# The last two convolution tiles, the layer norm and two output units of a conformer module, each done in two token streams on one core

## The chip, the cores and the metric

One core of a Trainium2 chip runs the whole program in one launch. The metric is device time in microseconds (us), the median of the runs.

## The reference, cut to what matters

The reference is a chain of transformer blocks at 256 tokens and width 1024. The change lies in layer 1 of the second block, which runs a conformer module over two sequences with shared weights: the latents and the context. They stand side by side as 512 columns, and this text calls each half of 256 columns a stream.

```python
def conformer_conv(h, w1, b1, dw, dwb, ln_g, ln_b, w2, b2):
    u = h @ w1 + b1
    a, g = jnp.split(u, 2, axis=-1)
    u = a * jax.nn.sigmoid(g)
    u = dwconv(u, dw) + dwb            # depthwise, 31 taps
    u = jax.nn.silu(layernorm(u, ln_g, ln_b))
    return u @ w2 + b2
```

## The kernel before, in words

**Layout.** Activations lie feature-major: 1024 features are 8 tiles (KT = 8) of 128 partitions, and the free axis holds 512 tokens, stream 0 in columns 0 to 255 and stream 1 in 256 to 511. A product keeps nearly full f32 accuracy with three matmuls per tile of the contraction (lines 1149 to 1151): weight hi with input hi, weight hi with input lo, weight lo with input hi. The weights come in units of 1024 by 256. SP loads a unit into one of 3 raw buffers; ACT makes its hi half in two pieces (L1359, L1360), and DVE the lo half (L1656, L1659). hi and lo have 2 slots, so unit j+2 can be split only when PE has finished with unit j.

**Order.** A planner written in Python (class Plan) writes one list of steps, and every engine goes through it in order and takes its own part of each step. So the list's order is each engine's queue. `beside` (L341) adds a share of `pace` to a credit after each tile of a product and, at 1, puts in one `condition` step (L329): 2 reductions of 1.2 us on DVE (L1735) over a buffer MW, which POOL loads anew after each. There are 192 such steps in the program, and later layers need their results.

**Depthwise convolution** (`cv_conv`, L1318). Per feature tile, copies of the padded input, shifted by 0 to 3 columns, lie on the four partition groups of UX; 16 DMAs per tile make them (`cv_spread`, and for tiles 6 and 7 `cv_spread_one`, 8 on SP and 8 on POOL). PE then does 8 taps for each of 4 groups of 32 output channels, 512 columns wide, in f32. ACT adds the bias into CV (L1581), DVE sums the tiles into SA (`cv_total`, L1997).

**Layer norm.** After tile 6 PE multiplies SA by a matrix of ones (L1334), after tile 7 it adds CV's last tile (L1337), and ACT copies the sum to RS as minus the mean (L1586). DVE centers the 8 tiles (L2002), ACT squares each (L1367) into one of two buffers, PE sums the squares with 8 matmuls by ones (L1179, L1182). ACT makes the reciprocal deviation by Ln and Exp (L1371, L1374), loads the table for Silu (L1352), and for each tile: DVE scales (L2007), ACT does Silu (L1591) and the hi copy (L1594), DVE the lo half (L2012).

**Output.** Four units 181 to 184 of cv_w2 give two output tiles each. ACT moves an output tile with its bias to AB (L1598), DVE adds it into the residual X (L1727), ACT squares it (L1367), POOL adds the squares into SA (L2084). The last unit, `close` (L394), runs stream 0 of both tiles, then stream 1, so that the norm of the following MLP can begin with stream 0: in the midst of stream 1 stand the two ones matmuls of stream 0 (`ones_part`, L1189 and L1192).

Of the kernel before, what the change touches and what calls it, by code (L numbers as in the profile page):

```python
# [1134 lines left out]
def tensor(e, w, m, p, acc):  # L1135
# [195 lines left out]
    def cv_total(k, u):  # L1331
        if k == KT - 2:
            w.wait_ge(("cv_add", k), free_of(6, u))
            e.matmul(m.ps[6][:, 0:512], ones, m.SA[:, :], start=True, stop=False).then_inc(*acc.says("cv_summed"))  # L1334
        if k == KT - 1:
            w.wait_ge(("cv_sum", k))
            e.matmul(m.ps[6][:, 0:512], ones, m.CV[:, k, :], start=False, stop=True).then_inc(  # L1337
                *acc.says(("acc", 6, u)))
# [893 lines left out]
```

## Time and profile before

| what | value |
|---|---|
| median of 3 runs | 3013.59 us (3011.38 to 3013.71) |
| the profiled execution's own time | 3015.04 us |
| its span, first to last instruction | 3013.1 us |
| mean granted TensorE clock | 0.985 |
| PE, DVE, ACT, POOL busy | 96%, 66%, 40%, 12% |
| the chain that ended last, by engine | PE 84%, DVE 9%, ACT 4%, DMA 1%, issue 1%, POOL 1% |

The profile is one execution; all times in it count from the start of its span. A row of the timeline gives start, length, engine, line and operation, and in brackets how long the engine was idle before and who ended that. The clock is told as a share of full speed: 1.00 is 2.4 GHz, 0.50 is 1.2 GHz.

### The profile page before, as it was taken

To read this page: it belongs to the slowest core of one execution; us is meant where nothing else is said; L and a number is where in the kernel's file an instruction comes from. 1 tells how busy PE (TensorE), PEld (TensorE's weight loads), DVE (VectorE), ACT (ScalarE), POOL (GpSimd) and SP (SyncE) were. 2 spreads that over 40 slices of the span, in tenths; PEclk is the share of its full clock that TensorE was granted. 3 is DMA by queue.
4 is the path that set the end of the run, shared out by engine and by line. 5 is a ranking of instruction groups with operands and counts; after the bars stand their busy time and mean duration, and the time that the engine had idled before them with its cause. 6 is when DMAs were issued, how large, how long until landed. Compare 5 with 4: busy or idle time off the path is not lost.

```text
span 3013.1 us, 42743 instructions
## 1 busy us (share of the span) xinstructions
PE 2899.0 (96%) x17730; PEld 2511.1 (83%) x17730; DVE 2000.8 (66%) x3252; ACT 1197.6 (40%) x1953; POOL 352.4 (12%) x545
## 2 busy tenths in 40 slices
PE   7999999989999989999999999999999999998998
PEld 7999998879977768888864888888888888876998
DVE  6776777658745557777644776777777667654665
ACT  5444444644444434223312632223234222443543
POOL 0000000000113220000122100001010000243000
PEclk9999999989999999999999999999999999999999
DMA  6444675347755523544464254553535545565453
GB/s 216 154 154 140 212 239 190 127 140 246 238 113 84 83 56 123 171 155 159 129 188 119 84 161 161 161 168 122 166 125 168 161 154 169 125 107 82 136 186 127
DMA packets 362275, 451.88 MB, mean 150 GB/s; under 512 B 12656, under 2 KB 332432, under 8 KB 362080
## 3 DMA queue, kind: packets, MB, share of 16 engines
q1 hardware_dynamic: 326976, 329.89, 33.7%
q0 software_dynamic: 34944, 118.65, 16.5%
q8 instruction: 140, 2.29, 0.3%
q10 hardware_dynamic: 160, 0.59, 0.1%
q14 instruction: 55, 0.45, 0.0%
HBM read 438.67 MB, written 1.05 MB: 146 GB/s over the span
## 4 chain that ended last, share of the span: by engine, by line
PE 84%; DVE 9%; ACT 4%; DMA 1%; issue 1%; POOL 1%; DVEq 0%; ACTq 0%; POOLq 0%
PE ps L1149 24%; PE ps L1151 24%; PE ps L1150 24%; PE ps L1327 2%; PE ps L1170 2%; PE ps L1171 1%; PE ps L1172 1%; DVE lo L1656 1%; PE ps L1314 1%; DVE NB L1690 1%; DVE lo L1659 1%; ACT hi L1359 1%; PE ps L1302 1%; PE ps L1282 1%; PE ps L1182 1%
## 5 line engine op out<-in xcount | busy, mean ns | idle before, releaser
L1149 PE MATMUL ps<-XN,hi 128*128 128x256 f32 (+1 forms) x3120 | 1037.3, 332 | 46.0 <-DVE XN L1903 11.3
L1150 PE MATMUL ps<-XN,hi 128*128 128x256 f32 (+1 forms) x3120 | 1020.1, 327 | 0.0
L1151 PE MATMUL ps<-XN,lo 128*128 128x256 f32 (+1 forms) x3120 | 1019.6, 327 | 0.0
L1149 PEld LDWEIGHTS ps<-XN,hi 128*128 128x128 f32 x3120 | 598.7, 192 | 122.4 <-issue 14.5
L1151 PEld LDWEIGHTS ps<-XN,lo 128*128 128x128 f32 x3120 | 598.9, 192 | 49.0
L1150 PEld LDWEIGHTS ps<-XN,hi 128*128 128x128 f32 x3120 | 599.4, 192 | 47.6
L1735 DVE CUSTOM_DVE_ANT_0 MX<-MW,C 128x1024 bf16<-128x1024 f32 x384 | 480.0, 1250 | 109.3 <-DMA MW<-in_mod_w 102.5
L1656 DVE TENSOR_TENSOR lo<-raw,hi 128x1024 fp32r<-128x1024 f32 (+1 forms) x313 | 383.9, 1227 | 242.7 <-ACT hi L1359 241.6
L1359 ACT ACTIVATE hi<-raw 128x1024 fp32r<-128x1024 f32 (+1 forms) x313 | 326.2, 1042 | 428.6 <-PE ps L1151 428.4
L1659 DVE TENSOR_TENSOR lo<-raw,hi 128x1024 fp32r<-128x1024 f32 (+1 forms) x313 | 380.3, 1215 | 0.0
L1149 PE MATMUL ps<-H,hi 128*128 128x512 f32 (+1 forms) x1072 | 380.2, 355 | 0.0
L1150 PE MATMUL ps<-H,hi 128*128 128x512 f32 (+1 forms) x1072 | 379.7, 354 | 0.0
L1151 PE MATMUL ps<-H,lo 128*128 128x512 f32 (+1 forms) x1072 | 379.7, 354 | 0.0
L1360 ACT ACTIVATE hi<-raw 128x1024 fp32r<-128x1024 f32 (+1 forms) x313 | 324.6, 1037 | 0.0
L2078 POOL DMA_DIRECT2D MW<-in_mod_w x192 | 103.0, 537 | 1451.0 <-DVE mod L1735 1341.6
L1150 PEld LDWEIGHTS ps<-H,hi 128*128 128x128 f32 x1072 | 202.7, 189 | 28.4
L1149 PEld LDWEIGHTS ps<-H,hi 128*128 128x128 f32 x1072 | 202.7, 189 | 28.2
L1151 PEld LDWEIGHTS ps<-H,lo 128*128 128x128 f32 x1072 | 202.7, 189 | 28.0
L1727 DVE SCALAR_TENSOR_TENSOR X<-ps,mod,X 128x256 f32<-128x256 f32 x244 | 108.2, 479 | 139.1 <-PE ps L1151 139.1
L2084 POOL TENSOR_TENSOR SA<-SA,NB 128x256 f32<-128x256 f32 (+1 forms) x69 | 70.4, 1020 | 812.5 <-ACT NB L1367 811.7
L1170 PE MATMUL ps<-hi,XN 128*128 128x256 f32 x512 | 151.5, 296 | 0.1
L1171 PE MATMUL ps<-lo,XN 128*128 128x256 f32 x512 | 145.5, 284 | 0.0
(239 smaller groups left out, 3402.8 us busy)
## 6 DMA issues: line engine op xcount, KB each, us to landing
raw<-in_mlp_w SPq DMA_DIRECT2D x128, 1024.0 KB, 5.4
MW<-in_mod_w POOLq DMA_DIRECT2D x192, 512.0 KB, 3.8
raw<-in_ffn_w_in SPq DMA_DIRECT2D x44, 1024.0 KB, 5.1
raw<-in_attn_w_in SPq DMA_DIRECT2D x36, 1024.0 KB, 4.8
raw<-in_na_wqkv SPq DMA_DIRECT2D x24, 1024.0 KB, 5.4
raw<-in_ffn_w_out SPq DMA_DIRECT2D x16, 1024.0 KB, 5.3
raw<-in_mlstm_w_in SPq DMA_DIRECT2D x12, 1024.0 KB, 5.0
raw<-in_cv_w SPq DMA_DIRECT2D x12, 1024.0 KB, 6.2
```

The source lines that it names most:

```text
L1149: e.matmul(out, whi, xhi, start=first, stop=False)
L1150: e.matmul(out, whi, xlo, start=False, stop=False)
L1151: i = e.matmul(out, wlo, xhi, start=False, stop=last)
L1170: e.matmul(out, xhi, hi[:, k, :], start=k == 0, stop=False)
L1171: e.matmul(out, xhi, lo[:, k, :], start=False, stop=False)
L1359: e.activation(hi[:, a:b], raw[:, a:b], ACT.Copy).then_inc(*high.says(("hi", j, 0)))
L1360: e.activation(hi[:, b:c], raw[:, b:c], ACT.Copy).then_inc(*high.says(("hi", j, 1)))
L1656: e.tensor_tensor(lo[:, a:b], raw[:, a:b], hi[:, a:b].bitcast(F32), ALU.subtract).then_inc(*low.says(("lo", j, 0)))
L1659: e.tensor_tensor(lo[:, b:c], raw[:, b:c], hi[:, b:c].bitcast(F32), ALU.subtract).then_inc(*low.says(("lo", j, 1), ("spent", j)))
L1727: e.scalar_tensor_tensor(out=m.X[:, j, a:b], in0=src[:, a:b], scalar=mod_of(m, gate, j, i), in1=m.X[:, j, a:b], op0=ALU.mult, op1=ALU.add) ...
L1735: e.tensor_tensor_reduce(out=m.MX[:, :], in0=m.MW[:, :], in1=m.C[:, s, :], scale=1.0, scalar=0.0, op0=ALU.mult, op1=ALU.add, accum_out=m.m ...
L2078: e.dma_start(m.MW[:, :], T["mod_w_2"][n // 48][n % 48 * P:(n % 48 + 1) * P, :]).then_inc(*sig["mw"].says(("mod_raw", n)))
```

## The change

Tiles 6 and 7 of the convolution, the mean, the centering, the squares, the variance and the normalisation are done per stream, with 256 columns each, and interleaved on PE: both tiles of stream 0, two taps of tile 6 of stream 1, the sum for the mean of stream 0, four more taps, the squares of stream 0, the last two taps, tile 7 of stream 1. Output units 181 and 182 multiply stream 0 of all tiles first (four PSUM banks held), with the mean and squares of stream 1 between, and stream 1 later. Squares go to four buffers in AB in place of two in NB. The splits of units 183 and 184 stand together ahead of the evacuation of unit 181. Units 181 and 182 now put in no condition step; `pace` in the last attention layer goes from 0.25 to 0.4. Line numbers of the new file are higher: 1210 to 1212 for 1149 to 1151, 1398 for the new convolution parts.

```diff
@@ -861,8 +861,7 @@

     def convolve(k):
         p.do("cv_conv", k, *p.bank())
-        p.do("cv_total", k, p.use(6)[1] if k == KT - 2 else p.bank_use[6])
-        p.flush()
+        p.do("cv_total", k)

     for c in range(4):
         def evac_g(t, b, u):
@@ -883,37 +882,94 @@
                 if k == KT - 4:
                     p.do("tables", LNEXP)
                 convolve(k)
-    for k in (KT - 2, KT - 1):
-        convolve(k)
-    p.sa_user = "cv_summed"
-    p.do("cv_mean", p.bank_use[6], p.rs_user)
-    for k in range(KT):
-        p.do("cv_center", k, p.norms)
-        p.square(k, 512, 1, "CV")
-        p.flush()
     p.flush()
-    p.rs_user = ("cv_center", KT - 1)
-    s = p.rstd(512)
+    used, rs_user, s = p.xn_used[1], p.rs_user, p.norms
+    p.norms += 1
+    x = ("cn", 0, 0, 512)
+
+    def unit(c):
+        j = p.take("cv_w2_2", 0, 0, KT, c * 256, 256)
+        p.reads(j, x)
+        return j
+
+    def products(j, banks, i, between):
+        for k in range(KT):
+            for t in range(2):
+                p.do("product", j, t, k, KT, banks[t], ("part", x, i), k == 0, k == KT - 1, i == 1, i == 1)
+            between(k)
+
+    def mean(i):
+        b, u = p.use(6 + i)
+        p.do("cv_mean_part", i, b, u, rs_user)
+        return b, u
+
+    def centered(i):
+        for k in range(KT):
+            p.do("cv_center_part", k, i)
+            p.do("cv_square_part", k, i)
+
+    def normed(i, ahead=2):
+        for k in range(KT + ahead):
+            if k < KT:
+                p.do("cv_norm_part", s, k, i)
+            if k >= ahead:
+                p.do("cv_silu_part", k - ahead, i, used)
+            if (k, i) == (ahead + 1, 0):
+                p.do("cv_conv_out", KT - 1, 1, *last)
+
+    j0 = unit(0)
+    left = [p.bank(), p.bank()]
+    for t in range(2):
+        p.do("cv_conv_part", KT - 2 + t, 0, 0, 8, *left[t])
+        p.do("cv_conv_out", KT - 2 + t, 0, *left[t])
+    p.do("cv_add_part", 0)
+    first, last = p.bank(), p.bank()
+    p.do("cv_conv_part", KT - 2, 1, 0, 2, *first)
+    sums = 6, p.bank_use[6] + 1
+    p.do("cv_total_part", 0, *sums)
+    mean(0)
+    p.do("cv_conv_part", KT - 2, 1, 2, 6, *first)
+    centered(0)
+    sums = p.use(6)
+    p.do("cv_ones_part", 0, 0, KT, *sums)
+    p.do("cv_conv_part", KT - 2, 1, 6, 8, *first)
+    p.do("cv_conv_out", KT - 2, 1, *first)
+    p.do("cv_add_part", 1)
+    p.do("rstd_part", s, 0, *sums, ("cv_center", KT - 1, 0))
     p.do("tables", SILU)
-    for k in range(KT + 2):
-        if k < KT:
-            p.do("cv_norm", s, k)
-        if k >= 2:
-            p.do("cv_silu", k - 2, p.last_unit)
+    p.do("cv_conv_part", KT - 1, 1, 0, 8, *last)
+    normed(0)
+    banks = [p.bank(), p.bank()], [p.bank(), p.bank()]
+    products(j0, banks[0], 0, lambda k: p.do("cv_total_part", 1, 7, p.bank_use[7] + 1) if k == 1 else None)
+    mean(1)
+    centered(1)
+    held, p.late = p.late, []
+    j1 = unit(1)
+    p.late = held + p.late
+    sums = p.use(7)
+    products(j1, banks[1], 0, lambda k: p.do("cv_ones_part", 1, 0, KT, *sums) if k == 3 else None)
     p.do("tables", LNEXP)
+    p.do("rstd_part", s, 1, *sums, ("cv_center", KT - 1, 1))
+    p.do("tables", SILU)
+    normed(1)
+    p.do("tables", LNEXP)
+    p.splits()
+    p.sa_user, p.sq_user = ("cv_totaled", 1), [("conv", KT - 1)] * 2
     p.rs_user = ("cn", 0, KT - 1)
-    for c in range(4):
-        def evac(t, b, u):
-            p.do("cv_out", 2 * c + t, t, b, u)
-            p.residual(2 * c + t, 512, (layer, 2), None, t, True)
-
-        def evac_part(j, t, i, b, u):
-            p.do("cv_out_part", j, t, i, b, u)
-
-        if c < 3:
-            p.linear("cv_w2_2", 0, 0, KT, c * 256, 256, ("cn", 0, 0, 512), evac, outer=c == 0, hold=c == 2)
-        else:
-            p.close("cv_w2_2", 0, 0, c * 256, ("cn", 0, 0, 512), (layer, 2), evac_part)
+
+    def evac(j, t, b, u):
+        p.do("cv_out", j, t, b, u)
+        p.residual(j, 512, (layer, 2), None, t, True)
+
+    def evac_part(j, t, i, b, u):
+        p.do("cv_out_part", j, t, i, b, u)
+
+    for c, j in enumerate((j0, j1)):
+        products(j, banks[c], 1, lambda k: None)
+        for t in range(2):
+            evac(2 * c + t, t, *banks[c][t])
+    p.linear("cv_w2_2", 0, 0, KT, 512, 256, x, lambda t, b, u: evac(4 + t, t, b, u), hold=True)
+    p.close("cv_w2_2", 0, 0, 768, x, (layer, 2), evac_part)


 def shortconv(p, layer):
@@ -996,7 +1052,7 @@
...
-    p.pace = 0.25
+    p.pace = 0.4
...
-        return ("xn", x[1][1], k, x[2]) if x[1][0] == "xn" else ready_of(x[1], k)
+        return (x[1][0], x[1][1], k, x[2]) if x[1][0] in ("xn", "cn") else ready_of(x[1], k)
...
+def squares_of(m, k):
+    return m.AB[:, k % 4 // 2, k % 2 * S:(k % 2 + 1) * S]
...
+    def cv_conv_part(k, i, j0, j1, b, u):
+        if j0 == 0:
+            w.wait_ge(("uxp", k), ("uxs", k), ("wd", k), free_of(b, u))
+        for j in range(j0, j1):
+            for g in range(4):
+                rows = m.UX[:, k // 2 % 2, g, k % 2, :].rearrange("p (s t) -> p s t", s=2)
+                f = e.matmul(m.ps[b][32 * g:32 * g + 32, 0:S], m.WD[:, k % 2, g * 8 + j, :],
+                             rows[:, i, 4 * j:4 * j + S], start=j == 0, stop=j == 7)
+        if j1 == 8:
+            f.then_inc(*acc.says(("acc", b, u), ("conv", k) if i else None))
+
+    def cv_total_part(i, b, u):
+        at = slice(i * S, (i + 1) * S)
+        w.wait_ge(("cv_add", KT - 2, i), free_of(b, u))
+        e.matmul(m.ps[b][:, 0:S], ones, m.SA[:, at], start=True, stop=False)
+        w.wait_ge(("cv_sum", KT - 1, i))
+        e.matmul(m.ps[b][:, 0:S], ones, m.CV[:, KT - 1, at], start=False, stop=True).then_inc(
+            *acc.says(("acc", b, u), ("cv_totaled", i)))
+
+    def cv_ones_part(i, k0, k1, b, u):
+        for k in range(k0, k1):
+            w.wait_ge(("cv_sq", k, i), free_of(b, u) if k == 0 else None)
+            e.matmul(m.ps[b][:, 0:S], ones, squares_of(m, k), start=k == 0, stop=k == KT - 1).then_inc(
+                *acc.says(("cv_ones", k, i), ("acc", b, u) if k == KT - 1 else None))

...
+    def cv_conv_out(k, i, b, u):
+        w.wait_ge(("acc", b, u))
+        e.activation(m.CV[:, k, i * S:(i + 1) * S], m.ps[b][:, 0:S], ACT.Identity,
+                     bias=param(m, "cv_dwb_2", k)).then_inc(*act.says(("free", b, u), ("cv_sum", k, i)))
+
+    def cv_mean_part(i, b, u, after):
+        w.wait_ge(("acc", b, u), after)
+        e.activation(m.RS[:, i * S:(i + 1) * S], m.ps[b][:, 0:S], ACT.Copy, scale=-1.0 / D).then_inc(
+            *act.says(("free", b, u), ("cv_mean", i)))
+
+    def cv_square_part(k, i):
+        w.wait_ge(("cv_center", k, i), ("cv_ones", k - 4, i) if k >= 4 else ("cv_ones", k + 4, 0) if i else None)
+        e.activation(squares_of(m, k), m.CV[:, k, i * S:(i + 1) * S], ACT.Square).then_inc(
+            *act.says(("cv_sq", k, i)))
+
+    def cv_silu_part(k, i, used):
+        at = slice(i * S, (i + 1) * S)
+        w.wait_ge(("cv_norm", k, i))
+        e.activation(m.CV[:, k, at], m.CV[:, k, at], ACT.Silu, bias=param(m, "cv_ln_b_2", k)).then_inc(
+            *act.says(("cv_silu", k, i)))
+        w.wait_ge(("cv_silu", k, i), used)
+        e.activation(m.XN[:, 0, k, at], m.CV[:, k, at], ACT.Copy).then_inc(*act.says(("cnhi", k, i)))

...
+    def cv_center_part(k, i):
+        at = slice(i * S, (i + 1) * S)
+        w.wait_ge(("cv_mean", i), ("cv_sum", k, i) if k >= KT - 2 else ("cv_sum", k))
+        if k == KT - 1:
+            w.wait_ge(("cv_totaled", i))
+        e.tensor_tensor(m.CV[:, k, at], m.CV[:, k, at], m.RS[:, at], ALU.add).then_inc(
+            *dve.says(("cv_center", k, i)))
+
...
```

PE's queue from convolution tile 4 on, in the module's middle, before (UX is the shifted input, NB and AB the squares, SA the sum of tiles, cst the ones):

```order
L1327 MATMUL ps<-UX,NB 32x512 x96
L1334 MATMUL ps<-SA,cst 128x512
L1327 MATMUL ps<-UX,NB 32x512 x32
L1337 MATMUL ps<-CV,cst 128x512
L1179 MATMUL ps<-SA,cst 128x512
L1182 MATMUL ps<-NB,cst 128x512 x7
L1149 MATMUL ps<-XN,hi 128x512
```

and now:

```order
L1388 MATMUL ps<-UX,NB 32x512 x64
L1398 MATMUL ps<-UX,NB 32x256 x72
L1406 MATMUL ps<-SA,cst 128x256
L1408 MATMUL ps<-CV,cst 128x256
L1398 MATMUL ps<-UX,NB 32x256 x16
L1414 MATMUL ps<-AB,cst 128x256 x8
L1398 MATMUL ps<-UX,NB 32x256 x40
L1210 MATMUL ps<-XN,hi 128x256
```

The 64 rows ahead are tiles 4 and 5. Of the 72 rows behind them 32 are tile 6 and 32 tile 7, both of stream 0, and 8 the first two taps of tile 6 of stream 1. So tile 7 moved ahead of the other stream's tile 6 and ahead of the first ones matmul.

How ACT's queue goes on behind the last Silu and hi copy, before (hi is a weight split, AB an output tile, X the residual):

```order
L1352 ACT_TABLE_LOAD
L1359 ACTIVATE hi<-raw 128x1024
L1360 ACTIVATE hi<-raw 128x1024
L1598 ACTIVATE AB<-ps,PV 128x512
L1367 ACTIVATE SA<-X 128x512
L1598 ACTIVATE AB<-ps,PV 128x512
L1367 ACTIVATE NB<-X 128x512
L1359 ACTIVATE hi<-raw 128x1024
```

and now:

```order
L1430 ACT_TABLE_LOAD
L1437 ACTIVATE hi<-raw 128x1024
L1438 ACTIVATE hi<-raw 128x1024
L1437 ACTIVATE hi<-raw 128x1024
L1438 ACTIVATE hi<-raw 128x1024
L1687 ACTIVATE AB<-ps,PV 128x512
L1445 ACTIVATE SA<-X 128x512
L1687 ACTIVATE AB<-ps,PV 128x512
L1445 ACTIVATE NB<-X 128x512
```

The two splits (units 183 and 184) now stand together ahead of the first output tile; before, one split stood there and the next only behind two output tiles.

## Rows read from the trace of the kernel before

**Rows 1.** The page: span, and busy time of the engines.
```profile
span 3013.1 us, 42743 instructions
...
PE 2899.0 (96%) x17730; PEld 2511.1 (83%) x17730; DVE 2000.8 (66%) x3252; ACT 1197.6 (40%) x1953; POOL 352.4 (12%) x545
```
**Rows 2.** Chain of waits, 1640 to 1662: start, length, what.
```profile
1642.52 1.14 PE ps L1337 x2
...
1645.72 1.13 PE ps L1179 x2
1646.84 8.09 PE ps L1182 x14
...
1656.33 1.28 ACT L1352
...
1657.62 0.73 ACT CV L1591
...
1659.78 0.79 PE ps L1149
```
**Rows 3.** Timeline of PE, tile 7 of the convolution (four column groups at once).
```profile
1634.63 7.07 PE L1327 MATMUL ps<-UX,NB 128*32 128x512 f32 x64
```
**Rows 4.** Timeline of ACT: the output of convolution tile 5.
```profile
1625.24 0.69 ACT L1581 ACTIVATE CV<-ps,PV 128x512 f32<-128x512 f32 x1 [6.18 <-PE ps L1327]
```
**Rows 5.** Tile UX, 1622 to 1634: issues (ns, first and last start) and landing.
```profile
L1095 SPq DMA_DIRECT2D UX<-U x8: 507/588/607, 1622.7 to 1627.3; - x8
...
DMA to landing us min/median/max: 4.5/4.9/5.8
```
**Rows 6.** By stretch: length, busy PE, PEld, DVE, ACT, POOL (records), clock, DMA.
```profile
1647.00:1650.40 3.40, 3.40 (x5) 1.30 (x4) 2.21 (x4) 0.96 (x2) 0.00 (x0) 0.50 0.00 0
...
1657.30:1664.00 6.70, 4.22 (x10) 3.35 (x11) 6.08 (x10) 6.53 (x11) 0.00 (x0) 0.50 0.00 1
```
**Rows 7.** Timeline of PE at full clock: products of 512 columns.
```profile
1664.38 0.39 PE L1151 MATMUL ps<-XN,lo 128*128 128x512 f32 x1
1664.62 0.39 PE L1149 MATMUL ps<-XN,hi 128*128 128x512 f32 x1
```
**Rows 8.** Timeline of PE: products of 256 columns; the ones matmuls of `close`.
```profile
1696.33 0.28 PE L1149 MATMUL ps<-XN,hi 128*128 128x256 f32 x1
1696.45 0.28 PE L1150 MATMUL ps<-XN,hi 128*128 128x256 f32 x1
...
1703.06 0.70 PE L1189 MATMUL ps<-SA,cst 128*128 128x256 f32 x2 [1.53 <-POOL SA L2091]
```
**Rows 9.** Groups by form, PE, 910 to 930: f32 matmuls of 256 columns.
```profile
L1314 PE MATMUL ps<-PT,VB 128*64 128x256 f32 x24 | 3.0, 388 | 0.0
```
**Rows 10.** Groups by form, ACT: operations of 256 columns.
```profile
L1392 ACT ACTIVATE XN<-NB,mod 128x256 fp32r<-128x256 f32 x96 | 48.3, 509 | 25.8 <-DVE NB L1690 25.8
...
L1379 ACT ACTIVATE NB<-X 128x256 f32<-128x256 f32 x24 | 10.0, 418 | 23.5 <-DVE X L1706 23.5
...
L1384 ACT ACTIVATE RS<-ps,eps 128x256 f32<-128x256 f32 x12 | 5.6, 466 | 8.0 <-PE ps L1192 8.0
```
**Rows 11.** Timeline of ACT, 1683 to 1704.
```profile
1683.86 0.69 ACT L1598 ACTIVATE AB<-ps,PV 128x512 f32<-128x512 f32 x1 [2.08 <-PE ps L1151]
1685.49 0.64 ACT L1367 ACTIVATE NB<-X 128x512 f32<-128x512 f32 x1 [0.95 <-DVE X L1727]
1686.03 1.04 ACT L1359 ACTIVATE hi<-raw 128x1024 fp32r<-128x1024 f32 x1
```
**Rows 12.** Timeline of DVE, 1683 to 1704.
```profile
1684.58 0.88 DVE L1727 SCALAR_TENSOR_TENSOR X<-AB,mod,X 128x256 f32<-128x256 f32 x2 [3.47 <-ACT AB L1598]
...
1693.06 1.96 DVE L1735 CUSTOM_DVE_ANT_0 MX<-MW,C 128x1024 bf16<-128x1024 f32 x1 [1.16 <-DMA MW<-in_mod_w]
...
1700.15 1.21 DVE L1659 TENSOR_TENSOR lo<-raw,hi 128x1024 fp32r<-128x1024 f32 x1
1701.29 0.47 DVE L1706 SCALAR_TENSOR_TENSOR X<-AB,mod,X 128x256 f32<-128x256 f32 x1
```

More of the change, by code:

```diff
@@ L1329, in cv_conv @@
         f.then_inc(*acc.says(("acc", b, u), ("conv", k)))
[L1331 to L1338, printed above, removed]
+    def cv_conv_part(k, i, j0, j1, b, u):
[20 more added lines that the diff above has]
+                *acc.says(("cv_ones", k, i), ("acc", b, u) if k == KT - 1 else None))
     w.wait_ge("consts")
@@ L1582, in cv_conv @@
             *act.says(("free", b, u), ("cv_sum", k)))
-    def cv_mean(u, after):
-        w.wait_ge(("acc", 6, u), after)
-        e.activation(m.RS[:, :], m.ps[6][:, :], ACT.Copy, scale=-1.0 / D).then_inc(
-            *act.says(("free", 6, u), "cv_mean"))
-    def cv_silu(i, unit):
-        w.wait_ge(("cv_norm", i))
-        e.activation(m.CV[:, i, :], m.CV[:, i, :], ACT.Silu, bias=param(m, "cv_ln_b_2", i)).then_inc(
-            *act.says(("cv_silu", i)))
-        w.wait_ge(("cv_silu", i), ("used", unit))
-        e.activation(m.XN[:, 0, i, :], m.CV[:, i, :], ACT.Copy).then_inc(*act.says(("cnhi", i)))
+    def cv_conv_out(k, i, b, u):
[17 more added lines that the diff above has]
+        e.activation(m.XN[:, 0, k, at], m.CV[:, k, at], ACT.Copy).then_inc(*act.says(("cnhi", k, i)))
     def cv_out(j, t, b, u):
@@ L1633, in scalar @@
         "na_turn": na_turn, "na_mix": na_mix, "cv_g": cv_g, "cv_conv": cv_conv,
-        "cv_mean": cv_mean, "cv_silu": cv_silu, "cv_out": cv_out, "sc_c": sc_c, "sc_halves": sc_halves,
+        "cv_conv_out": cv_conv_out, "cv_mean_part": cv_mean_part, "cv_square_part": cv_square_part,
+        "cv_silu_part": cv_silu_part, "cv_out": cv_out, "sc_c": sc_c, "sc_halves": sc_halves,
         "mlp_up": mlp_up})
@@ L1992, in cv_a, with cv_total @@
             *dve.says(("wd", k)))
-    def cv_total(k, u):
-        if 0 < k < KT - 1:
+    def cv_total(k):
+        if k:
             w.wait_ge(("cv_sum", k), ("cv_add", k - 1) if k > 1 else None)
@@ L1998, in cv_total, with cv_add_part, cv_norm_part, cv_silu_part @@
                 *dve.says(("cv_add", k)))
-    def cv_center(k, s):
-        w.wait_ge("cv_mean", ("cv_sum", k))
-        e.tensor_tensor(m.CV[:, k, :], m.CV[:, k, :], m.RS[:, :], ALU.add).then_inc(
-            *dve.says(("cv_center", k), ("x", s, k)))
-    def cv_norm(s, k):
-        w.wait_ge(("rstd", s), ("cv_center", k))
-        e.scalar_tensor_tensor(out=m.CV[:, k, :], in0=m.CV[:, k, :], scalar=param(m, "cv_ln_g_2", k),
-                               in1=m.RS[:, :], op0=ALU.mult, op1=ALU.mult).then_inc(*dve.says(("cv_norm", k)))
-    def cv_silu(i, unit):
-        w.wait_ge(("cnhi", i))
-        e.tensor_tensor(m.XN[:, 1, i, :], m.CV[:, i, :], m.XN[:, 0, i, :].bitcast(F32), ALU.subtract).then_inc(
-            *dve.says(("cn", 0, i)))
+    def cv_add_part(i):
+        at = slice(i * S, (i + 1) * S)
+        w.wait_ge(("cv_sum", KT - 2, i), ("cv_add", KT - 3))
+        e.tensor_tensor(m.SA[:, at], m.SA[:, at], m.CV[:, KT - 2, at], ALU.add).then_inc(
+            *dve.says(("cv_add", KT - 2, i)))
+    def cv_center_part(k, i):
+        at = slice(i * S, (i + 1) * S)
+        w.wait_ge(("cv_mean", i), ("cv_sum", k, i) if k >= KT - 2 else ("cv_sum", k))
[3 more added lines that the diff above has]
+            *dve.says(("cv_center", k, i)))
+    def cv_norm_part(s, k, i):
+        at = slice(i * S, (i + 1) * S)
+        w.wait_ge(("rstd", s, i), ("cv_center", k, i))
+        e.scalar_tensor_tensor(out=m.CV[:, k, at], in0=m.CV[:, k, at], scalar=param(m, "cv_ln_g_2", k),
+                               in1=m.RS[:, at], op0=ALU.mult, op1=ALU.mult).then_inc(*dve.says(("cv_norm", k, i)))
+    def cv_silu_part(k, i, used):
+        at = slice(i * S, (i + 1) * S)
+        w.wait_ge(("cnhi", k, i))
+        e.tensor_tensor(m.XN[:, 1, k, at], m.CV[:, k, at], m.XN[:, 0, k, at].bitcast(F32),
+                        ALU.subtract).then_inc(*dve.says(("cn", 0, k, i), ("cn", 0, k) if i else None))
     def sc_v(c, t, b, u):
```

7 lines of the change are left out of this document (4 added, 3 removed).

## The prediction

> **What bounds the kernel now.** I read the page, then the chain of waits across the convolution module, then the timelines of the stretches that the change touches. The page has PE busy for 2899.0 of 3013.1 us [rows 1], so only stretches in which PE waits or runs slowly can give time back. In the conformer there is one. PE ends tile 7 near 1641.7 [rows 3], and the chain then alternates: a ones matmul at 1642.52, the squares from 1645.72 to 1654.93, a Silu table, Silu at 1657.62, the first product at 1659.78 [rows 2]. PE has nothing in hand for 0.8, 2.1 and 4.9 us of it, and its clock stood at 0.50 in two pieces: over the squares after the wait of 2.1 us, and over the first ten products after the wait of 4.9 us [rows 6].
>
> The sum is made against the profiled execution (span 3013.1, own time 3015.04). The median is 3013.59, so I take differences worked out in the trace and subtract them from the median.
>
> **1. A new wait in front (bad).** Convolution tile 5 ends just before its output copy at 1625.24 [rows 4]. Before, tile 6 followed for 6.9 us, then a ones matmul, and tile 7 began at 1634.63 [rows 3]. Now tile 6 of stream 0 takes half: 16 steps of four column groups. An f32 matmul of 256 columns in column groups took 3.0/12 = 0.25 us with its tail [rows 9]; half of tile 7's 7.07/16 is 0.22 [rows 3]. I take 0.216, so 3.45 us, and tile 6 ends at 1628.6. Then the queue wants tile 7 of stream 0, whose shifted input is not there: SP issues the last of its 8 copies at 1627.3, and the slowest took 5.8 us to land [rows 5], 1633.1; were it the fastest, 4.5, it would be 1631.8. Nothing upstream of these copies changes. PE stands for 4.5 us (bounds 3.2 and 4.5). Before, this landing was covered by tile 6's second stream. Tile 7 of stream 0 runs from 1633.15 to 1636.6.
>
> **2. The first stream gets ready earlier (good).** From 1636.6, with about 0.05 us per handover: tail and output copy 0.7, to 1637.3; by 1637.46 PE has done two taps (0.86). Two ones matmuls of 2 x 0.216 each give 1638.33; the mean with its tail 0.6; center and square 0.9. PE does four taps (1.73) until 1640.06, so the first squares are there. Eight ones matmuls of 0.43 follow without a gap, since four buffers let ACT (0.42 a square [rows 10]) run ahead: 1643.5. The last two taps 0.86, to 1644.4. ACT's queue wants the output of tile 6 of stream 1 first (until 1645.0), then Ln 0.47 [rows 10] and Exp 0.42 with handovers, 1645.9, then the table load of 1.28 [rows 2]. Silu begins at S = 1647.2 in place of 1657.62: **10.4 us earlier**. PE does tile 7 of stream 1 meanwhile, until 1647.8.
>
> **3. The rest of the module is longer (bad).** Count from S. Silu with bias is 0.51 [rows 10], the hi copy is issued 0.33 later, so ACT makes a tile of 256 columns per 0.86 us; PE needs 6 x 0.12 = 0.72 for it [rows 8]. ACT sets the pace: first product at S+1.46, unit 181 of stream 0 done at S+8.6 (one tile output copy of 0.4 among the Silus). Four tiles of unit 182 (2.9), eight ones (3.46), to S+14.95; four tiles more, to S+17.8. The deviation of stream 1 is ready at S+16.1, the second Silu table at S+17.4, and its first product at S+18.84: PE idles 1.0. Unit 181 ends at S+25.6, unit 182 at S+31.36.
>
> ACT's queue now holds both splits ahead of the first output tile, and the second needs unit 182's slot. So: splits until S+33.45, DVE's lo half until S+34.9, and only then six output tiles, each 2.17 us by the cycle from 1683.86 to 1686.03 [rows 11, 12]. That makes 47.9, less the 0.7 by which the first copy overlaps the lo half: S+47.2. A split follows (1.9), and from the second lo piece (S+49.45) to the first ones matmul of `close` it took 1703.06 - 1700.15 = 2.91 [rows 8, 12]: **S+52.35**. PE, with units 183 (10.9) and 184 (5.8 and 1.1), is there at S+49.1 and waits 3.25 us, where it waited 1.53 [rows 8]. Before, the same matmul stood at 1703.06 - 1657.62 = S+45.45. So 6.9 of the 10.4 us are handed back, and the second ones matmul follows in 0.6 in place of 0.73. **At full clock the gain is 3.6 us.** Behind it the program is as before.
>
> Within this are 96 products of 512 columns turned into 192 of 256. At full clock one starts every 0.23 us with 512 columns [rows 7] and every 0.12 with 256 [rows 8]: 96 x 0.013 = 1.3 us. The Trainium skill (TensorE: Matmul & The Clock Gate, Back-to-back issue gap) gives a stream of weight loads and matmuls 131 ns per matmul at 512 columns and 81 at 128. An estimate half way, 106 ns for 256 columns, makes the split 96 x 81 ns = 7.8 us. The rows measure the same thing here and disagree; they decide.
>
> **4. Clock.** The wait of 4.5 us is like the one of 4.9, after which PE ran at 0.50 until 1664 and lost 10 x 0.2 us [rows 6, 7]. I take 1.8 lost in tile 7 of stream 0, all on the path (bounds 0 and 2.1). For the wait of 3.25 us the nearest rows disagree: 1.53 us left the clock alone, 2.1 us (after another 0.8) did not [rows 2, 6]. A fall costs the 15 products behind it 15 x 0.093 = 1.4 us. I take half, 0.7 (bounds 0 and 1.4).
>
> **5. Conditions.** Two condition steps leave this module, whose DVE rows (1.96 and 1.2 us each pair [rows 12]) are not in my S+52. One each goes to the two MLPs and the last attention layer, one leaves the short convolution. MLP stages are covered by PE. In the last attention layer a step of 2.5 us on DVE costs 0 to 2.5; the two that stand there now cost PE nothing visible, so 0.
>
> **Sum:** 3.6 - 1.8 - 0.7 = 1.1 us. Predicted time 3013.6 - 1.1 = **3012.5 us**, chance 0.50.
>
> **Rivals.**
> - *The tail does not bind.* If output tiles overlap better than 2.17 us each (ACT's next copy needs no wait for DVE), the 3.25 us at the end vanish: gain 6.9, **3006.7**. For it: DVE and ACT are far from full. Against: both queues are strictly in order and the square of each tile stands between. Chance 0.20; this is the case of faster by over 0.2% (6.0 us).
> - *No clock fall, and the copies land at 1631.8:* gain 3.6 + 1.2, **3008.8**, chance 0.10.
> - *Both falls in full, and the attention layer pays for its third condition:* 3.6 - 1.8 - 1.4 - 2.5 = -2.1, **3015.7**, chance 0.08.
> - *The clock stays down (slower).* The wait for the tile 7 copies drops the clock to 1.2 GHz, and the handovers after it keep it there until S. Then tile 7 costs 3.45 more and the 0.86, 1.73, 3.46 and 0.86 us behind 6.9 more, the ones for the mean 0.86: 3.6 - 11.2 = -7.6, **3021.2**. It decides from the point where PE's own work is the longest piece between 1636 and S, which it is. Against: PE is nearly full from 1633 on, and it came back within 4.3 us of work at 1664 [rows 6]. The skill's page (section HAM oscillation) tells of kernels in which every tile's wait drops the clock anew; that is this case. Chance 0.10.
> - *The split is dear as the page has it:* 6.5 more than in my sum, **3019.0**, chance 0.02. It would also need rows 8 to be wrong.
> - *It does not do what it says:* four buffers bring nothing, squares stay at the 1.15 us per tile of 1646.84 to 1654.93 [rows 2]; with half the columns at least 0.6, 1.3 us more: 3013.8. I count it in the forecast.
>
> **Range.** From the tail rival, 3006.7, to the third condition with about 2 us for handovers that I rounded: 3006.5 to 3017.5. It leaves out the slow clock and half of what lies beyond the first rival. Chances: faster by over 0.2% (what a measurement of this kernel can tell from no change) 0.20, within it 0.68, slower 0.12.
>
> **What would show it.** In the changed profile: a PE wait of 3 to 5 us ending near 1633 on a UX copy and clock 0.50 behind it; Silu at 1647 to 1649; a second wait of about 1 us near S+18; ACT from the double split to the last output tile without a pause of its own, and PE's wait before the `close` ones longer than 1.53. I am wrong if tile 7 starts at 1628.6, or if the first ones of `close` comes before S+50.

## The result, and the profile after

The changed kernel takes **3019.81 us** (median of 13 runs, 3017.85 to 3022.38), the kernel before in the same session 3013.71 (13 runs, 3008.60 to 3020.37): ratio 1.002, 95% interval 1.0012 to 1.0027. It is **slower by 6 us**, where I had forecast 1.1 us faster and a range that ended at 3017.5. The span of the profiled execution is 3017.7 us, before 3013.1 [rows 1]. The page of the changed kernel, span and busy time of the engines:

```profile
span 3017.7 us, 43298 instructions
...
PE 2900.3 (96%) x17974; PEld 2525.6 (84%) x17974; DVE 2005.9 (66%) x3277; ACT 1203.9 (40%) x1984; POOL 348.2 (12%) x545
```

PE is busy for 1.3 us more, so most of the loss is waiting. The profiles also differ ahead of the stretch that the change touches: weight split 181, that of the first output unit, starts between 1600.2 and 1605.3 us in the thirteen profiles of this study. So I read every profile from the start of split 181, by the starts of later splits (ACT's rows `hi<-raw`, counted from 0) and of a few other rows. All in us from split 181:

| profile | first Silu | first output tile | ones of `close` | split 186 | split 266 | split 272 | split 278 | split 312 |
|---|---|---|---|---|---|---|---|---|
| before | 56.57 | 71.25 | 102.01 | 120.80 | 1002.78 | 1071.33 | 1160.45 | 1392.26 |
| after | 48.38 | 81.98 | 103.35 | 123.69 | 1006.50 | 1078.66 | 1164.06 | 1395.80 |

Split 186 is behind the module, 266 behind the close of the MLP of layer 2, 272 and 278 in the last attention layer, 312 at the end of the last MLP.

**The front went as worked out.** PE's row of tile 7 of stream 0, and the stretch behind the wait (length, busy PE, PEld, DVE, ACT, POOL with records, clock, DMA share, GB/s):

```profile
1634.00 5.35 PE L1398 MATMUL ps<-UX,NB 128*32 128x256 f32 x64 [4.35 <-DMA UX<-U]
```
```profile
1634.40:1637.80 3.40, 3.40 (x39) 2.18 (x32) 0.65 (x2) 0.00 (x0) 0.00 (x0) 0.50 1.06 395
```

The wait for the copies of tile 7, 4.35 us, took the place of the covered landing, and the clock stood at 0.50 behind it, so that the tile took 5.35 us where I had 3.45 at full clock. ACT's timeline at the first Silu:

```profile
1649.16 1.28 ACT L1430 ACT_TABLE_LOAD   x1
1650.45 0.51 ACT L1680 ACTIVATE CV<-CV,PV 128x256 f32<-128x256 f32 x1
```

From split 181 the Silu is 8.2 us earlier; my 10.4 less 1.8 for the clock were 8.6.

**The end did not.** Between Silu and the ones matmul of `close` lie 54.97 us, where I had 52.35 and the kernel before 45.44. DVE's timeline over the six output tiles, then POOL's:

```profile
1685.61 0.87 DVE L1817 SCALAR_TENSOR_TENSOR X<-AB,mod,X 128x256 f32<-128x256 f32 x2
1687.76 0.88 DVE L1817 SCALAR_TENSOR_TENSOR X<-AB,mod,X 128x256 f32<-128x256 f32 x2 [1.28 <-ACT AB L1687]
1689.91 1.44 DVE L1817 SCALAR_TENSOR_TENSOR X<-AB,mod,X 128x256 f32<-128x256 f32 x2 [1.27 <-ACT AB L1687]
1692.63 1.43 DVE L1817 SCALAR_TENSOR_TENSOR X<-AB,mod,X 128x256 f32<-128x256 f32 x2 [1.27 <-ACT AB L1687]
1695.34 1.43 DVE L1817 SCALAR_TENSOR_TENSOR X<-AB,mod,X 128x256 f32<-128x256 f32 x2 [1.28 <-ACT AB L1687]
1698.05 1.44 DVE L1817 SCALAR_TENSOR_TENSOR X<-AB,mod,X 128x256 f32<-128x256 f32 x2 [1.27 <-ACT AB L1687]
```
```profile
1689.39 1.28 POOL L2185 TENSOR_TENSOR SA<-SA,NB 128x512 f32<-128x512 f32 x1 [57.49 <-ACT NB L1445]
1692.10 1.29 POOL L2185 TENSOR_TENSOR SA<-SA,NB 128x512 f32<-128x512 f32 x1 [1.42 <-ACT NB L1445]
1694.81 1.29 POOL L2185 TENSOR_TENSOR SA<-SA,NB 128x512 f32<-128x512 f32 x1 [1.42 <-ACT NB L1445]
```

The first two tiles are 2.15 us apart, as I took them for all. From the third on it is 2.71: the residual pair takes 1.44 in place of 0.88 [rows 12], each time while an add of POOL runs. PE's timeline at `close`, and the clock in two stretches (columns as above):

```profile
1699.49 0.28 PE L1212 MATMUL ps<-XN,lo 128*128 128x256 f32 x1
1705.42 1.22 PE L1250 MATMUL ps<-SA,cst 128*128 128x256 f32 x2 [5.64 <-POOL SA L2192]
```
```profile
1697.00:1702.00 5.00, 2.77 (x24) 2.57 (x22) 2.21 (x3) 3.49 (x6) 2.57 (x2) 1.00 0.00 0
...
1702.70:1709.40 6.70, 3.98 (x14) 3.57 (x15) 2.10 (x3) 2.08 (x5) 0.72 (x1) 0.50 0.52 157
```

PE was done with units 183 and 184 at S+49.3 (I had 49.1; S is the first Silu), and waited 5.64 us in place of my 3.25. The clock was at 0.50 until 1709.4. From the second lo piece of the last split, at 1702.51, to the ones matmul it took 2.91 us, as before: the loss lies ahead of that piece.

**And something was lost far behind the module**, where I had expected nothing: 0.8 us more between splits 186 and 266 than before, and 3.6 more between 266 and 272. (Between 186 and 224 the change is 0.5 us quicker, between 224 and 266 it is 1.3 slower.) PE's timeline in the last attention layer, the first context matmul, whose row was the same before but with 1.42 us of wait:

```profile
2668.48 1.88 PE L1363 MATMUL ps<-cst,PB 128*128 128x128 f32 x8 [3.46 <-DVE PB L2043]
```

DVE's timeline shows a condition step in its queue ahead of two lo halves and of the rows (PB) that this matmul waits for:

```profile
2658.30 1.75 DVE L1825 CUSTOM_DVE_ANT_0 MX<-MW,C 128x1024 bf16<-128x1024 f32 x1
2660.09 1.23 DVE L1825 CUSTOM_DVE_ANT_0 MX<-MW,C 128x1024 bf16<-128x1024 f32 x1
```

It is the second step of the layer, 49.7 us behind split 266. In the kernel before it stands 41.3 us behind it, early enough to be done before those rows are due. The third stands at 2696.24, behind the wait, and costs nothing visible there: from split 272 to 278 the change takes 85.4 us, as the profiles with two steps do (85.2 to 85.7, but for that of before; see experiment 11).

### The profile page after: what moved, and what is told of

The parts are those of the page before. It is cut to its first block, busy times and chain, and to the rows that moved or that the text cites. A ratio compares the mean times of both kernels' runs of the same rounds, so it can differ in the third digit from the quotient of the medians.

```text
span 3017.7 us, 43298 instructions
## 1 busy us (share of the span) xinstructions
PE 2900.3 (96%) x17974; PEld 2525.6 (84%) x17974; DVE 2005.9 (66%) x3277; ACT 1203.9 (40%) x1984; POOL 348.2 (12%) x545
## 4 chain that ended last, share of the span: by engine, by line
PE 83%; DVE 9%; ACT 4%; issue 1%; DMA 1%; POOL 1%; DVEq 0%; ACTq 0%; POOLq 0%
PE ps L1210 24%; PE ps L1212 24%; PE ps L1211 24%; PE ps L1231 2%; PE ps L1232 1%; PE ps L1233 1%; DVE lo L1746 1%; DVE lo L1749 1%; PE ps L1375 1%; PE ps L1388 1%; ACT hi L1437 1%; DVE NB L1780 1%; PE ps L1363 1%; PE ps L1343 1%; DMA MW<-in_mod_w 1%
## 5 line engine op out<-in xcount | busy, mean ns | idle before, releaser
L1210 PEld LDWEIGHTS ps<-XN,hi 128*128 128x128 f32 x3152 | 605.8, 192 | 117.7 <-issue 14.2
L1212 PEld LDWEIGHTS ps<-XN,lo 128*128 128x128 f32 x3152 | 605.8, 192 | 47.4
L1211 PEld LDWEIGHTS ps<-XN,hi 128*128 128x128 f32 x3152 | 606.6, 192 | 46.1
L1712 ACT ACTIVATE H<-NB 128x512 fp32r<-128x512 f32 (+1 forms) x128 | 74.1, 579 | 181.1 <-DVE NB L2150 181.1
```

The lines of the kernel that those rows point to most:

```text
L1210: e.matmul(out, whi, xhi, start=first, stop=False)
L1211: e.matmul(out, whi, xlo, start=False, stop=False)
L1212: i = e.matmul(out, wlo, xhi, start=False, stop=last)
L1712: e.activation(m.H2[:, q % 2, 0, k, 0:n], rl, ACT.Copy).then_inc(*act.says(("h2hi", layer, r)))
```

## The experiments

Each is read by the table's landmarks, times from the start of split 181, and, where it has more than one run, by the ratio to runs of the kernel before on the same chip. Landmarks come from one profile each.

**1. Tail.** The split of unit 184 behind the output tiles of units 181 and 182.

```diff
-    p.splits()
+    if p.late:
+        p.late.pop(0)()
```

> The split of unit 184 stands behind the four output tiles of units 181 and 182, no longer ahead of them. Theory A (ACT's queue with two splits ahead of the first output tile delays all of the module's end): the first output copy starts right behind unit 181, some 7 us earlier than 1684, POOL's adds and the residual sums are done before unit 184, PE's wait before the ones matmul of the close shrinks from over 3 us to 1.5 or less, the clock stays at 1.00 there, and the time falls by 5 to 6 us against the changed kernel, to within 1 us of the kernel before. Theory B (the wait for the copies of tile 7 at 1634 is the main loss): the time falls by less than 2 us. Theory C (the moved condition steps cost it, in the last attention layer): no change.

3018.18 us (11 runs, 3015.81 to 3022.56), before 3015.82 (27 runs), ratio 1.0009 (1.0000 to 1.0017). First output tile at 76.05, split 186 at 119.89: 3.8 us earlier than in the change. PE's wait at `close`:

```profile
1701.49 1.03 PE L1251 MATMUL ps<-SA,cst 128*128 128x256 f32 x2 [2.25 <-POOL SA L2193]
```

The double split was on the path. But I had expected 5 to 6 us, a wait of 1.5 us or less and no fall of the clock; the ratios give 3.3 us, and the wait of 2.25 us was still followed by a fall, to 0.50 from 1702.

**2. Convolution order.** Stream 1 of tile 6 ahead of stream 0 of tile 7, to fill the wait for its copies.

```diff
-    for t in range(2):
-        p.do("cv_conv_part", KT - 2 + t, 0, 0, 8, *left[t])
-        p.do("cv_conv_out", KT - 2 + t, 0, *left[t])
+    p.do("cv_conv_part", KT - 2, 0, 0, 8, *left[0])
+    p.do("cv_conv_out", KT - 2, 0, *left[0])
+    p.do("cv_conv_part", KT - 2, 1, 0, 8, *first)
+    p.do("cv_conv_out", KT - 2, 1, *first)
+    p.do("cv_conv_part", KT - 1, 0, 0, 8, *left[1])
+    p.do("cv_conv_out", KT - 1, 0, *left[1])
```

> Stream 1 of convolution tile 6 is done ahead of stream 0 of tile 7, in the wait for tile 7's shifted input. Theory B (that wait and the fall of the clock behind it are the main loss): the wait shrinks from 4.35 us to 0.9, the clock stays at 1.00, Silu of stream 0 begins 2.5 to 3.5 us earlier and the time falls by that much against the changed kernel. Theory A (the end of the module binds): Silu begins earlier all the same, and the whole of the gain reaches the end, since the module's end is a chain that begins at Silu; it then adds to that of the other experiment. Rival: the convolution wait was free because the first stream waits for the sum over tiles on DVE in any case: under 1 us.

3019.16 us (11 runs), ratio 1.0009 (1.0000 to 1.0018). The wait for the copies is 1.10 us and the clock stays at 1.00:

```profile
1632.31 4.52 PE L1399 MATMUL ps<-UX,NB 128*32 128x256 f32 x80 [1.10 <-DMA UX<-U]
```

First Silu at 45.51, split 186 at 120.32: 3.4 us earlier than in the change.

**3. POOL.** Five adds of the squares behind the module take 8 columns of 512; this leaves most of the squares out of that norm's sum.

```diff
+            n = 8 if s == 9 else n
             e.tensor_tensor(m.SA[:, 0:n], m.SA[:, 0:n], m.SQ[:, i % 2, 0:n], ALU.add).then_inc(
```

> The changed kernel with POOL's adds of squares behind the conformer cut to 8 columns in place of 512 (the norm of the MLP behind it is then computed from a part of the squares). Theory (POOL's adds and DVE's residual sums slow one another when they run side by side): each pair of residual sums of output tiles 2 to 5 takes 0.88 us, not 1.44, one output tile every 2.17 us, not 2.71, and the ones matmul of the close comes 2.2 us earlier behind the first Silu (52.8 in place of 54.95 us). Rival (DVE is slow there for another reason, as what ACT or PE read and write): the pairs stay at 1.44 us.

One run, 3017.14 us. Timelines of DVE and POOL:

```profile
1690.79 0.88 DVE L1817 SCALAR_TENSOR_TENSOR X<-AB,mod,X 128x256 f32<-128x256 f32 x2 [1.28 <-ACT AB L1687]
1692.94 0.88 DVE L1817 SCALAR_TENSOR_TENSOR X<-AB,mod,X 128x256 f32<-128x256 f32 x2 [1.28 <-ACT AB L1687]
```
```profile
1690.27 0.20 POOL L2186 TENSOR_TENSOR SA<-SA,NB 128x8 f32<-128x8 f32 x1 [57.91 <-ACT NB L1445]
```

All six pairs take 0.88 and stand 2.15 us apart; the wait at `close` falls from 5.64 to 3.30, which is my 3.25, and split 186 comes 2.0 us earlier. POOL's adds are what stretched the output tiles.

**4. Tail and early tap matrices.** As 1, and DVE makes the tap matrices of tiles 6 and 7 behind the input tiles of both (in the change each tile's taps stand behind its input, so tile 7's input and the copies that follow it come later).

```diff
+            if c < 3:
+                p.do("cv_taps", 2 * c + t)
...
-        p.linear("cv_w1_2", 0, 0, KT, c * 256, 256, x, evac_a)
+        p.linear("cv_w1_2", 0, 0, KT, c * 256, 256, x, evac_a, quiet=c == 3)
+        if c == 3:
+            for t in range(2):
+                p.do("cv_taps", 6 + t)
+                p.beside()
```

> Both the later split of unit 184 and an earlier input for tile 7: DVE writes the input of tiles 6 and 7 before it makes their tap matrices, so that the copies for tile 7 are issued some 10 us earlier. Theory A and B together: no wait for UX, PE goes from tile 6 to tile 7 of stream 0 at 1629.7; the sum over tiles on DVE (1634.6 in the changed kernel, behind a split) becomes what the first stream waits for, Silu begins about 4 us earlier than in the changed kernel; the time is 8 to 10 us below the changed kernel and 2 to 4 us below the kernel before. If only theory A holds: about the time of the kernel before.

3012.77 us (11 runs, 3009.32 to 3017.43), ratio **0.9986 (0.9978 to 0.9995)**, faster than the kernel before. PE's timeline has one unbroken row over stream 0 of tiles 6 and 7 and the two taps of stream 1 behind them; the wait that is left is for DVE:

```profile
1629.28 7.95 PE L1405 MATMUL ps<-UX,NB 128*32 128x256 f32 x144
1638.88 0.70 PE L1413 MATMUL ps<-SA,cst 128*128 128x256 f32 x2 [1.65 <-DVE SA L2102]
```

First Silu at 43.86, split 186 at 115.61, 5.2 us earlier than before. The last attention layer still has its 3.6 us of loss (266 to 272 in 72.20 us).

**5. Condition steps early.** The change, with the two condition steps that left the module made up for at the first two places of the MLP behind it, so that all later ones stand where they stood before. The credit is set back so that the count comes out, and the pace in the last attention layer is the old one.

```diff
+        elif self.owed and not hold:
+            self.owed -= 1
+            self.condition()
...
     conformer(p, 1)
+    p.owed, p.credit = 2, p.credit - 0.68
...
-    p.pace = 0.4
+    p.pace = 0.25
```

> The changed kernel, in which the two condition steps that left the convolution module are made up for at the first two places that the MLP behind it offers, so that from there on every condition step stands where it stood before, with the pace of before in the last attention layer. The module itself is as in the change. Theory (the shifted condition steps cost about 0.7 us at the end of the MLPs, where one of them now stands between two residuals of the closing units): counted from the start of weight split 181, split 266 comes at 1005.8 in place of 1006.5, and the wait in front of the ones matmul of the last close is back at 0.3 us; the last attention layer starts its work as before. Rival (the 0.7 us come from elsewhere, for instance the clock): 1006.5 as in the change, whatever the condition steps do. Second rival (two more condition steps in the MLP cost there what they saved elsewhere): split 200 later than in the change by over 0.5 us. Time about 0.7 us under the change's, which one run does not resolve; the split times do.

One run, 3019.47 us. Split 200 comes at 275.30, in the change at 269.82: the second rival, and with 5.5 us dearer than I had put it. PE waits three times (0.49, 2.10, 2.06 us) for a lo half that stands in DVE's queue behind the added steps, and DVE itself for their weights. DVE's timeline:

```profile
1756.08 1.23 DVE L1829 CUSTOM_DVE_ANT_0 MX<-MW,C 128x1024 bf16<-128x1024 f32 x1 [2.06 <-DMA MW<-in_mod_w]
1757.23 0.08 DVE L1829 DVE_READ_ACCUMULATOR2_ANT mod<- 128x1 f32 x1
1757.35 1.22 DVE L1829 CUSTOM_DVE_ANT_0 MX<-MW,C 128x1024 bf16<-128x1024 f32 x1
1758.50 0.08 DVE L1829 DVE_READ_ACCUMULATOR2_ANT mod<- 128x1 f32 x1
1758.50 1.22 DVE L1750 TENSOR_TENSOR lo<-raw,hi 128x1024 fp32r<-128x1024 f32 x1
```

Yet it shows what the places of the condition steps are worth later. From split 224 to 266 the kernel before takes 468.82 us, this one 468.82, the change 470.10 (0.57 of it in the short convolution, 0.71 at the close of the MLP of layer 2). From 266 to 272 it takes 68.55, before 68.55, the change 72.16.

**6. Three edits** (tail, early taps, condition steps as in 5), expected before 5 was known.

> The changed kernel with three edits together: the split of unit 184 behind the four output tiles of units 181 and 182 (as in the first experiment on the tail), the tap matrices behind the input tiles of the last two convolution tiles, and the condition steps put back where they stood before. Theory: the module ends 5.2 us earlier than in the kernel before (as with the first two edits alone), the conditions give 0.7 more: ratio to the kernel before 0.998, 0.9973 to 0.9988, so about 6 us faster. Rival (what the first two edits gave was noise of the stretch in front of the module): ratio 0.9995 to 1.0005.

3012.28 us (11 runs, 3008.89 to 3020.02), before 3013.57 (21 runs), ratio 1.0000 (0.9991 to 1.0009). I had expected 0.998. Not the rival's reason: split 186 is at 113.50, 7.3 us ahead of before, but split 200 at 265.53, 1.6 ahead. Of what the module gained, 5.7 us were handed back by the early condition steps.

**7. The same, with the order of 2.**

> As the version with three edits, and with stream 1 of tile 6 ahead of stream 0 of tile 7 as well. Theory (with the inputs landed early there is no wait left that this order could fill, so it only puts 3.45 us of work in front of stream 0, of which the 1.65 us that PE waits behind tile 7 are the most that it can cover): first Silu 1 to 2 us later than with the three edits, end of the module 0 to 2 us later, ratio between 0.998 and 0.999. Rival (stream 1 is what sets the end of the module, and gets ready earlier by this order): end of the module 1 us earlier or more.

3014.25 us (10 runs), ratio 1.0005 (0.9996 to 1.0014). First Silu at 44.20, 1.0 later; split 186 at 118.16, 4.7 later than in 6, more than the 0 to 2 expected: the clock fell at 1648 and 1702, which it did not in 6. With the copies landed the order has nothing to fill.

**8. The price of 256 columns**, by itself: before, with 30 more units of the MLP of layer 2 multiplied stream by stream.

```diff
-                     streams=(0, 1) if q + c == 0 and n == 512 else None)
+                     streams=(0, 1) if (q + c == 0 or layer == 2) and n == 512 else None)
...
-                         quiet=q == 3 and c == 3, hold=(q, c, n) == (3, 2, 512))
+                         quiet=q == 3 and c == 3, hold=(q, c, n) == (3, 2, 512),
+                         streams=(0, 1) if layer == 2 and n == 512 else None)
```

> The kernel before, in which 30 more units of the MLP of layer 2 are multiplied in two halves of 256 columns: 480 products of 512 columns become 960 of 256. It measures the price of that split by itself, which the change pays on 96 products. Theory (rows of the kernel before: one product of 512 columns per 0.2264 us, one of 256 per 0.120 us): 480 x 0.0136 = 6.5 us more, time 3020. Rival (the estimate from the page on TensorE, 81 ns more for each product that is split): 480 x 0.081 = 39 us more, time 3052. A second rival (PE is not what bounds the MLP, so that nothing shows): no difference.

3031.90 us (4 runs, 3031.32 to 3034.38), ratio 1.0063 (1.0050 to 1.0077). My count was wrong by three: a product step issues three matmuls (hi and lo), so 480 steps are 1440 matmuls. With the right count the rows give 1440 x 0.0136 = 19.6 us, and the estimate from the Trainium skill's figures (TensorE: Matmul & The Clock Gate, Back-to-back issue gap) 1440 x 0.081 = 117. Split 266 came 18.8 us later than before: 0.013 us for each matmul that is split. PE's groups over that MLP show it full, with matmuls of 256 columns alone:

```profile
L1150 PE MATMUL ps<-H,hi 128*128 128x256 f32 x492 | 139.2, 283 | 0.0
L1151 PE MATMUL ps<-H,hi 128*128 128x256 f32 x492 | 139.2, 283 | 0.0
L1152 PE MATMUL ps<-H,lo 128*128 128x256 f32 x491 | 139.0, 283 | 0.0
```

**9. Condition steps late.** The change, with the two steps among the down units of the MLP's second and fourth quarter; credit and pace as in 5.

```diff
+        elif self.owed and not hold and self.parts >= (125, 111)[self.owed - 1]:
+            self.owed -= 1
+            self.condition()
```

> The changed kernel, with the two missing condition steps made up for late in the MLP behind the module (among the down units of its second and fourth quarter) in place of at its first tiles, and with every condition step from condition 130 on where it stood before. Theory (the second rival of the earlier experiment was right: at the first tiles DVE is the late engine, and two more steps of 2.5 us there cost 5.5 us; among the down units DVE has room): counted from the start of weight split 181, split 200 at 269.8 as in the change, split 266 at 1005.5 (1006.5 in the change), split 272 at 1074 in place of 1078.7, since the last attention layer has two condition steps again and PE's wait in front of its first context matmul is 1.6 us in place of 3.3; split 312 at 1391.5 to 1392.5 (1395.8). Time 3014 to 3017 with the noise in front of the module. Rival (the attention layer's 3.6 us have nothing to do with the condition step): split 272 at 1077.5 or later.

One run, 3012.40 us. Split 200 at 269.78, 266 at 1005.63, 272 at 1074.18, 312 at 1390.20: nothing is lost in the MLP, and the later places are those of before. The first context matmul of the last attention layer:

```profile
2664.09 1.09 PE L1367 MATMUL ps<-cst,PB 128*128 128x128 f32 x8 [1.42 <-DVE PB L2047]
```

DVE's timeline, the second condition step of the layer, now 40.9 us behind split 266 again and done before the rows of this matmul are due:

```profile
2647.14 1.22 DVE L1829 CUSTOM_DVE_ANT_0 MX<-MW,C 128x1024 bf16<-128x1024 f32 x1
```

So the place of the condition steps in that layer was the cause: 2.0 us of wait, and about 1.6 of slow clock behind it. The wait is 3.46 to 3.60 us in the five profiles with a step 49.7 to 49.8 us behind split 266 (after, 1 to 4), and 1.41 to 1.66 in the eight with it at 40.9 to 41.7 (before, 5 to 11). The edit takes the third step away and moves the second back; no run does one without the other, but the third, by its time in the change, comes after the loss. With 3012.40 us the run is also below the 3014 to 3017 that I expected.

**10. Tail, early taps, condition steps late.**

> The tail edit, the early tap matrices and the condition steps made up for late. Theory: module ends 7.3 us earlier than in the kernel before (split 186 at 113.5 from split 181, as with the three edits), nothing lost in the MLP behind it (split 200 at 260 to 261), split 312 at 1382 to 1383 in place of 1392.3; ratio to the kernel before 0.9975 (0.9965 to 0.9985). Rival (the room in the MLP is used up, and what is gained in the module is handed back at the close of the MLP): split 266 over 998, ratio 0.9985 to 1.

**3008.86 us** (11 runs, 3005.62 to 3013.67), before 3013.20 (15 runs), ratio **0.9987 (0.9978 to 0.9996)**. Split 200 at 261.06, 266 at 997.06, 312 at 1382.97, as expected; split 186, at 114.70 where I expected 113.5, had a fall of the clock ahead of it (1699). It has the lowest median of the study, 4.3 us under the kernel before and, by the two ratios, about 10 under the change. But the gain is half of the 0.9975 that I expected, and the ratio is no better than that of experiment 4 (0.9986), whose split 312 comes 4.8 us later: these runs don't show at the end what the condition steps' places give in the profiles. The landmarks have it 7.2 us under experiment 11. Some of the difference lies ahead of them. Split 181 starts at 1602.8 to 1605.3 us in the five profiles with early taps and at 1600.2 to 1603.0 in the eight others, 2.5 us apart on the mean. From split 140 to 181 all thirteen take 485.9 to 486.0 us, so it comes from a stretch in which PE and ACT have the same instructions in all. Whether the edit brings it on or chance does is open.

**11. Control.** The kernel before with the early taps alone.

> The kernel before, with only the tap matrices of tiles 6 and 7 behind the input tiles of both, so that SP's copies for tile 7 are issued earlier. Theory (before, the second stream of tile 6 covered the landing): first Silu and split 186 as before within 0.3 us, 56.6 and 120.8 from split 181, so that the early inputs are worth something only once the streams are split. Rival (they were late before too, somewhere the profile puts on another engine): split 186 at 119.8 or less. It is also a second profile of the last attention layer as it was before, with waits of PE of about 1.7 and 2.1 us at its two later context matmuls: if the clock falls there again, split 272 to split 278 takes 89 us, else 85.5.

One run, 3016.05 us. First Silu at 56.57, as before to 0.01, split 186 at 120.41: landing earlier is worth nothing as long as the second stream of tile 6 covers it. From split 272 to 278 it takes 85.5 us, as the change and all other experiments do (85.2 to 85.7), and the profile of before 89.1. In that profile the clock fell twice there, by stretch (columns as above):

```profile
2705.20:2708.50 3.30, 3.30 (x18) 3.30 (x17) 0.84 (x2) 0.60 (x1) 0.00 (x0) 0.50 0.49 130
2749.50:2752.90 3.40, 3.40 (x18) 3.40 (x17) 1.00 (x2) 0.60 (x1) 0.51 (x1) 0.50 0.84 277
```

So the profile of the kernel before holds 3.6 us that its other executions need not have, and hid as much of what the moved condition step costs.

## Why the prediction was wrong, point by point

- **Step 1, the wait for tile 7: right.** 4.35 us for 4.5. Experiments 2 and 4 take it away in two ways, 11 shows that it was covered before.
- **Step 2, the earlier Silu: right.** 8.2 us for 8.6 with the clock.
- **Step 3, output tiles at 2.17 us each: the first term that failed.** I took the cycle from the first output tile of the kernel before. There no residual pair stands beside an add of POOL, because splits and condition steps stand between the tiles; now nothing does. Four of the six pairs run beside an add and take 1.44 us, their tiles 2.71, 2.2 us in all. That is most of the 2.6 by which the ones matmul of `close` came late, and experiment 3 gives 2.3 of the wait back (5.64 to 3.30). The row that spoke against it was on my own list: DVE's condition row took 1.96 us [rows 12], and POOL ran an add beside it. Timelines of POOL and DVE in the kernel before, one such row that began ahead of an add, the next one beside it:

```profile
1686.21 1.54 POOL L2084 TENSOR_TENSOR SA<-SA,NB 128x512 f32<-128x512 f32 x1 [3.06 <-ACT NB L1367]
...
1692.66 1.28 POOL L2084 TENSOR_TENSOR SA<-SA,NB 128x512 f32<-128x512 f32 x1 [2.96 <-ACT NB L1367]
```
```profile
1685.38 1.22 DVE L1735 CUSTOM_DVE_ANT_0 MX<-MW,C 128x1024 bf16<-128x1024 f32 x1
...
1686.64 2.19 DVE L1735 CUSTOM_DVE_ANT_0 MX<-MW,C 128x1024 bf16<-128x1024 f32 x1
```

- **Step 3, the double split: right** in kind; experiment 1 gives 3.4 us of wait back by taking it apart. The part ahead of it came out too: a wait of 0.93 us at S+18.9, for my 1.0 at S+18.84.
- **Step 3, the price of 256 columns: right.** 0.013 us for each matmul, 18.8 us over 1440; the estimate from the Trainium skill (TensorE: Matmul & The Clock Gate, Back-to-back issue gap) would have been 117 there.
- **Step 4, the clock: mis-sized at the second gap.** At the first, tile 7 took 1.9 us more than at full clock, for my 1.8. For the second gap I took half of 1.4. From the ones matmul of `close` to split 186 it took 20.35 us, before 18.79 (1703.06 [rows 8] to split 186), so 1.6 for my 0.7. The waits of 5.64 us in the change and experiments 2, 5 and 9 were all followed by a fall, and so was the one of 3.30 in experiment 3, as long as the 3.25 that I had.
- **Step 5, conditions at 0: the second term that failed**, and the largest. I had bounds of 0 to 2.5 and took 0, since the two steps that stood in the last attention layer cost nothing visible. I had counted steps and not looked at their places. In the change the second step stands 8.4 us later, in DVE's queue ahead of what the first context matmul waits for, and that costs 3.6 (experiments 5 and 9), over my upper bound, which had left out the clock; the third step itself costs nothing visible. The other moved steps cost another 1.3 us in the short convolution and at the close of the MLP of layer 2, which I had called covered by PE.
- **The sum.** In the module 2.9 us slower in place of 1.1 faster (0.4 from the front, 2.6 from Silu to `close`, 0.9 from the clock), then 1.3 and 3.6 behind it, less 0.5 between splits 186 and 224: 7.3 us slower, where the medians are 6.1 apart, 3.6 to 8.1 by the interval. The two profiles' table shows only 3.5, for the reason of experiment 11.
- **The rivals.** That of both falls and a third condition step, 3015.7 at a chance of 0.08, named the right layer, with too small a price and the wrong step, and without what the output tiles lost. The squares were not slow (3.72 us for eight ones matmuls, for my 3.46), and experiment 8 has the dear split out. The clock came back after each gap, 3.4 us after it fell behind tile 7's wait and 6.8 us at `close`, so the rival in which it stays down is out. "The tail does not bind" is out too: the six tiles were strictly in order.

## What to carry to other kernels

When streams are split, what a later stream's work used to cover (a landing copy, a weight split in front of the output) becomes the path: move the producer of the early stream's last input and the splits first; here these two edits turned 0.2% slower into 0.14% faster (experiment 4). A cycle time holds for the neighbours it was read with, also on engines off the path: ask which rows will now run at the same time. And background steps placed by a pace move everywhere when a module has fewer places for them; compare their positions to the end of the program, and put them where DVE has room.
